# Hybrid encoder step on one Trainium2 core: low parts on VectorE, splits and sums issued ahead, the pooling mixer in two banks, filler matmuls in three norms

## What is computed

```python
h = rms_norm(x, norm_mix_g) * (1 + sc1) + sh1          # shift, scale, gate: silu(c) @ ada_w + ada_b
z = h @ w_in                                           # all mixers' inputs and the branch gates
oa = dsa_attention(...)   # indexer scores, top-k keys, softmax over them, 6 heads
ob = fox_attention(...)   # decay by cumulative sums of log-forget values, 6 heads
oc = pool_mixer(...)      # trailing means over 2, 4, 8, 16 frames minus the token, 64x64 map per group, scale
merged = sum_i sigmoid(gate_i) * (branch_i @ w_br_i)
x = x + g1 * (merged @ w_out)
h = rms_norm(x, norm_ffn_g) * (1 + sc2) + sh2
x = x + g2 * (swiglu(h) if layer == 0 else moe_ffn(h))  # moe: top 2 of 8 experts
```

## Time and profile before

| | |
|---|---|
| Runs | 2292.15, 2295.45, 2296.94 us |
| Profiled execution, its own time | 2291.52 us |
| Its span, first to last instruction | 2289.7 us |
| TensorE busy | 2173.7 us, 95% |
| Chain of work that ended last | TensorE 91%, VectorE 4%, DMA 2%, ScalarE 2%, issue 1% |
| VectorE / ScalarE / GpSimd busy | 34% / 25% / 13% |
| Mean granted TensorE clock | 0.964 of full speed |
| HBM traffic over the span | 147 GB/s |

### The profile page before, as it was taken

How to read it: one execution, slowest core, us unless ns; L and a number is a source line. 1 busy time by engine, 2 the same in 40 slices (tenths; PEclk the granted TensorE clock), 3 DMA queues, 4 the chain that set the end, 5 groups by cost and what they waited for, 6 DMA issues and landing times.

```text
span 2289.7 us, 38283 instructions
## 1 busy us (share of the span) xinstructions
PE 2173.7 (95%) x16051; PEld 2021.6 (88%) x16051; DVE 767.3 (34%) x1675; ACT 563.5 (25%) x1108; POOL 306.2 (13%) x194
## 2 busy tenths in 40 slices
PE   5999998999999999997999998999899999999995
PEld 3787998777989999997898997778699999999995
DVE  4032922545443333332308614545400000000024
ACT  4223321331232122223233312322411111111002
POOL 2223442000200000002224430003200000000001
PEclk8999998989999999998999998979999999999998
DMA  9674221501342243223624220012768877887783
GB/s 311 211 241 137 74 92 37 189 1 60 104 108 81 76 112 87 58 87 128 218 93 131 75 73 15 1 39 77 263 196 258 270 235 221 255 275 239 223 268 114
DMA packets 309445, 328.25 MB, mean 143 GB/s; under 512 B 7550, under 2 KB 276492, under 8 KB 308764
## 3 DMA queue, kind: packets, MB, share of 16 engines
q1 hardware_dynamic: 302144, 303.41, 42.1%
q0 software_dynamic: 5632, 18.41, 2.4%
q10 hardware_dynamic: 1548, 4.71, 0.5%
HBM read 310.29 MB, written 26.16 MB: 147 GB/s over the span
## 4 chain that ended last, share of the span: by engine, by line
PE 91%; DVE 4%; DMA 2%; ACT 2%; issue 1%; POOL 0%; DVEq 0%; SPq 0%; POOLq 0%; ACTq 0%
PE ps L1008 17%; PE ps L1363 17%; PE ps L1316 17%; PE ps L954 10%; PE ps L1344 8%; PE ps L881 5%; PE ps L1167 3%; PE ps L1153 3%; PE ps L1131 2%; PE ps L901 2%; PE ps L1073 1%; DMA slots<-in_ada_w 1%; PE ps L1391 1%; PE ps L1293 1%; PE ps L1328 1%
## 5 line engine op out<-in xcount | busy, mean ns | idle before, releaser
L1008 PE MATMUL ps<-hH,slotsR 128*128 128x272 f32 x1536 | 294.3, 291 | 3.9 <-ACT oT L1561 3.9
L1363 PE MATMUL ps<-hR,wR 128*128 128x272 f32 x2016 | 253.0, 288 | 1.8 <-DVE wR L2054 1.8
L1363 PEld LDWEIGHTS ps<-hR,wR 128*128 128x128 f32 x2016 | 252.7, 188 | 2.0 <-issue 2.0
L1008 PEld LDWEIGHTS ps<-hH,slotsR 128*128 128x128 f32 x1536 | 244.6, 191 | 4.5 <-issue 4.5
L730 POOL TENSOR_TENSOR slotsR<-slots,slotsR 128x1024 fp32r<-128x1024 f32 x64 | 154.9, 2440 | 610.8 <-ACT slotsR L1495 610.8
L1008 PE MATMUL ps<-hL,slotsR 128*128 128x272 f32 x768 | 223.3, 291 | 0.0
L954 PE MATMUL ps<-wz,hH 128*128 128x250 f32 (+1 forms) x680 | 194.8, 286 | 11.6 <-DVE hL L1779 7.3
L954 PE MATMUL ps<-slotsR,hH 128*128 128x250 f32 (+1 forms) x720 | 202.1, 281 | 0.0
L954 PE MATMUL ps<-wz,hL 128*128 128x250 f32 (+1 forms) x680 | 189.4, 279 | 0.0
L1316 PE MATMUL ps<-hg,slots 128*128 128x160 f32 x1280 | 177.3, 300 | 1.5 <-ACT hg L1657 0.6
L1316 PEld LDWEIGHTS ps<-hg,slots 128*128 128x128 f32 x1280 | 174.5, 190 | 3.5 <-issue 3.5
(11 more groups left out here) (364 smaller groups left out, 3399.6 us busy)
## 6 DMA issues: line engine op xcount, KB each, us to landing
slots<-in_w_in SPq DMA_DIRECT2D x24, 1024.0 KB, 5.2
slots<-in_ada_w SPq DMA_DIRECT2D x18, 1024.0 KB, 8.2
slots<-in_w_in SPq DMA_DIRECT2D x18, 1000.0 KB, 5.3
slots<-in_moe_w_gate SPq DMA_DIRECT2D x16, 1024.0 KB, 6.1
slots<-in_moe_w_up SPq DMA_DIRECT2D x16, 1024.0 KB, 8.0
w_more<-in_moe_w_gate SPq DMA_DIRECT2D x16, 1024.0 KB, 5.5
w_more<-in_moe_w_up SPq DMA_DIRECT2D x16, 1024.0 KB, 8.0
ada_x<-in_ada_w SPq DMA_DIRECT2D x15, 1024.0 KB, 7.1
```

What stands on the lines that cost most here:

```text
L1008: last = mm(ps[:, 2 * out_pair + a, 0:HALF], w[:, c], r[:, n], start=(k == i == 0), stop=(k == KD - 1 and i == 2))
L1363: last = mm(ps[:, 2 * out_pair + h, 0:HALF], wR[:, buf, a, k * P:(k + 1) * P], rhs(k, b)[:, c], start=(first and k == 0 and i == 0), stop= ...
```

## The change

1. **Start of layer 0.** The low parts of z block (0,0) move from GpSimd to VectorE (`proj_low`), at k = 1 and k = 4 of a loop that now interleaves `sample_affine` and `hidden_low`; ScalarE makes only the first half's high part ahead of norm 0 and the second after k = 2. The loads of `past` on GpSimd's queue move behind the low parts of block (0,1).
2. **z block (0,1), both layers.** ScalarE makes its high parts right after norm 2L.
3. **Layer 1's ada weights** take the three places in another order (3, 4, 5), so that the first fills wait for `x_upd` alone.
4. **Fillers.** `keep_busy` issues bf16 128x128 matmuls of an identity into bank 5, whose result is not read: 16 between the two halves of `norm_sums`, 14 ahead of `norm_scales`, 36 behind it, in norms 1, 2 and 3 (198 in all).
5. **Gates.** The wait for all 16 relu'd scores ahead of the first gate becomes 14 ahead of gate 0 and 16 ahead of gate 1.
6. **Pooling mixer.** Two buffers and two banks (5 and 6); VectorE copies tile t+1 before it scales tile t.
7. **Output product.** Its low parts move from GpSimd to VectorE (eight per layer), and `add_square(d-1)` stands ahead of `residual(d)` (in the FFN's second half too).
8. **End.** The second additions of token tiles 0 and 1 stand ahead of the last `y_copy`.

```diff
@@ buffers
-        pooled = qk[0:HD, 0:512]
+        pooled = [qk[0:HD, 0:512], oTf[0:HD, 1024:1536]]
@@ ada places
-        ... + [(5, 3, 4)[i % 3] for i in range(4 * ADA_LATER + 2 * ADA_FIRST)]
+        ... + [(5, 3, 4)[i % 3] for i in range(2 * (ADA_LATER + ADA_FIRST))] \
+            + [(3, 4, 5)[i % 3] for i in range(2 * ADA_LATER)]
@@ GpSimd
-                        low(("z", L), it, j)
+                        if L or it or j:
+                            low(("z", L), it, j)
+                        if L == it == 0 and j == 1:
+                            load_past()
...
-                with pool.Fori(0, 2) as it:
-                    for j in range(2):
-                        low(("out", L), it, j)
@@ TensorE, norm_sums and norm_scales
                     if i:
+                        if n:
+                            keep_busy(16)
                         pe.wait_ge(sq_ready, KD * (n + 1))
...
+            def keep_busy(count):
+                for _ in range(count):
+                    mm(ps[:, 5, 0:P], identb[:, :], identb[:, :], start=True, stop=True)
...
+                if n:
+                    keep_busy(14)
                 b0 = 2 * scale_pair(n)
...
                 last.then_inc(scale_ready, 1)
+                if n:
+                    keep_busy(36)
@@ TensorE, gates
-                pe.wait_ge(is_relu, 16 * (L + 1))
...
+                            if g < 2:
+                                pe.wait_ge(is_relu, 16 * L + 14 + 2 * g)
@@ TensorE, pooling mixer
+                pe.wait_ge(cum_evac, L + 1)
...
-                    if t:
-                        pe.wait_ge(po_evac, TILES * L + t)
+                    if t >= 2:
+                        pe.wait_ge(po_evac, TILES * L + t - 1)
...
-                            last = mm(ps[:, 5, pr * P:pr * P + r], poolw[:, g, :], pooled[:, g * P:g * P + r],
+                            last = mm(ps[:, 5 + t % 2, pr * P:pr * P + r], poolw[:, g, :], pooled[t % 2][:, g * P:g * P + r],
@@ ScalarE
-                    proj_high(("z", 0), 0, 0)
+                    proj_high(("z", 0), 0, 0, (0,))
...
-                norm(2 * L)
+                norm(2 * L, None if L else lambda: proj_high(("z", 0), 0, 0, (1,)))
+                proj_high(("z", L), 0, 1)
@@ VectorE
+            def proj_low(name, it, j, half):
+                high, low_part, w = proj_parts(name, j, it)
+                c = slice(half * 4 * w, (half + 1) * 4 * w)
+                dve.wait_ge(pw_high, proj_halves(name, it, j) + half)
+                V.tensor_tensor(low_part[:, c], slots[:, ring.slot(name, j), c], high[:, c].bitcast(FP), ALU.subtract)\
+                    .then_inc(pw_split, 1)
...
+                    for k in range(KD + 2):
+                        if k < KD:
+                            sample_affine(0, k)
+                        if k in (1, 4):
+                            proj_low(("z", 0), 0, 0, k // 4)
+                        if k >= 2:
+                            hidden_low(0, k - 2)
...
+                    if d >= KD - 2:
+                        proj_low(("out", L), 0, 0, d - (KD - 2))
                 merged_low(KD - 1)
+                for half in range(2):
+                    proj_low(("out", L), 0, 1, half)
...
+                    if d:
+                        add_square(2 * L + 1, d - 1)
                     dve.wait_ge(r_ready, KD * L + d + 1)
                     residual(d % 4, d, M_G1)
-                    if d:
-                        add_square(2 * L + 1, d - 1)
+                    if d in (1, 3):
+                        for half in range(2):
+                            proj_low(("out", L), 1, d // 2, half)
...
                     for d in range(KD):
+                        if d == KD - 1:
+                            add_second(0, 0)
+                            add_second(0, 1)
                         y_copy(before, d)
```

More of the change, by code:

```diff
@@ L518, in proj_parts @@
             return slotsR[:, 3 - j % 2, :], slotsR[:, j % 2, :], 2 * P
-        ada_places = [0, 1, 2, 3, 4, 5, 3, 4] + [(5, 3, 4)[i % 3] for i in range(4 * ADA_LATER + 2 * ADA_FIRST)]
+        ada_places = [0, 1, 2, 3, 4, 5, 3, 4] + [(5, 3, 4)[i % 3] for i in range(2 * (ADA_LATER + ADA_FIRST))] \
+            + [(3, 4, 5)[i % 3] for i in range(2 * ADA_LATER)]
         def ada_chunk(n):
@@ L718, in _, with load_past @@
                     pool.wait_ge(ot_evac, L * NTM)
[L719 to L721 removed]
+                def load_past():
+                    pool.dma_start(past[:, 0:192], t_in["cache_a_kvi"][L, 0].rearrange("t c d -> t (c d)")).then_inc(past_loaded, 16)
+                    pool.dma_start(past[:, 192:960], t_in["cache_b_kv"][L, 0].rearrange("t c h d -> t (c h d)")).then_inc(past_loaded, 16)
+                    pool.dma_start(past[:, 960:966], t_in["cache_b_logf"][L, 0]).then_inc(past_loaded, 16)
+                if L:
+                    load_past()
                 def low(name, it, j):
@@ L927, in _ @@
                     pe.wait_ge(vt_evac, 2)
+                    pe.wait_ge(memsets, 3)
                 def indexer_columns(i):
@@ L1460, in ffn_high, with norm @@
                 A(wR[:, w, 0, 0:n], slots[:, j % NSLOT, c0:c0 + n], ACT.Copy).then_inc(w_high, 1)
-            def norm(n):
+            def norm(n, weights_too=None):
                 act.wait_ge(mod_ready, n + 1)
@@ L1480, in norm @@
                         high(k - 1)
+                    if weights_too and k == 2:
+                        weights_too()
                 if n < 3:
@@ L1484, in _, with proj_high @@
             for L in range(DEPTH):
-                def proj_high(name, it, j):
+                def proj_high(name, it, j, parts=(0, 1)):
                     high, _, w = proj_parts(name, j, it)
@@ L1492, in proj_high @@
                         act.wait_ge(block_begun, released)
-                    for half in range(2):
+                    for half in parts:
                         c = slice(half * 4 * w, (half + 1) * 4 * w)
@@ L1837, in _ @@
                     ada_finish(0, 0, 16, ADA_FIRST)
-                    for k in range(KD):
-                        sample_affine(0, k)
-                    for k in range(KD):
-                        hidden_low(0, k)
+                    for k in range(KD + 2):
[5 more added lines that the diff above has]
+                            hidden_low(0, k - 2)
                 tmpf = oT[:, :, :].rearrange("p k n -> p (k n)")
@@ L1953, in _ @@
                 last.then_inc(cum_evac, 1)
-                for t in range(TILES):
-                    r = ROWS[t]
-                    dve.wait_ge(pm_ready, TILES * L + t + 1)
-                    if t:
-                        dve.wait_ge(po_ready, TILES * L + t)
-                    v4 = lambda ap: ap.rearrange("p (g n) -> p g n", g=4)[:, :, 0:r]
-                    V.tensor_copy(v4(pooled), v4(ps[0:HD, t, :])).then_inc(pm_evac, 1)
-                    dve.wait_ge(po_ready, TILES * L + t + 1)
-                    for pr in range(2):
-                        last = V.tensor_scalar(oT[:, 6 + pr, tok(t)], ps[:, 5, pr * P:pr * P + r],
-                                               vecT[:, L, V_PSC + pr:V_PSC + pr + 1], None, ALU.mult)
-                    last.then_inc(po_evac, 1)
+                for t in range(TILES + 1):
+                    if t < TILES:
+                        r = ROWS[t]
+                        dve.wait_ge(pm_ready, TILES * L + t + 1)
+                        if t >= 2:
+                            dve.wait_ge(po_ready, TILES * L + t - 1)
+                        v4 = lambda ap: ap.rearrange("p (g n) -> p g n", g=4)[:, :, 0:r]
+                        V.tensor_copy(v4(pooled[t % 2]), v4(ps[0:HD, t, :])).then_inc(pm_evac, 1)
+                    if t:
+                        b, r = t - 1, ROWS[t - 1]
+                        dve.wait_ge(po_ready, TILES * L + b + 1)
+                        for pr in range(2):
+                            last = V.tensor_scalar(oT[:, 6 + pr, tok(b)], ps[:, 5 + b % 2, pr * P:pr * P + r],
+                                                   vecT[:, L, V_PSC + pr:V_PSC + pr + 1], None, ALU.mult)
+                        last.then_inc(po_evac, 1)
                 for i, (kind, t) in enumerate(at_groups):
@@ L2240, in _ @@
                         if d >= 0:
+                            if it and d:
+                                add_square(2, d - 1)
                             dve.wait_ge(unit_done[1], it * nb + (n0 * nb + FB + d + 1))
@@ L2243, in _ @@
                             residual((d + 2) % 4, d, M_G2)
-                            if it and d:
-                                add_square(2, d - 1)
                     if it + 1 < HALVES:
                         ffn_low(it + 1, 0, 0)
+                    else:
+                        add_square(2, KD - 2)
                     dve.wait_ge(unit_done[1], it * nb + (n0 * nb + FB + KD))
```

22 lines of the change are left out of this document (10 added, 12 removed).

## The result

The changed kernel takes 2270.15 us (median of four runs, 2263.33 to 2273.15) against 2296.19 us for the kernel before beside it; the ratio is 0.9873 with a 95% interval of 0.9856 to 0.989, that is 25 to 33 us less. Two later sets of runs of the same kernel gave 0.9884 (0.9867 to 0.99) and 0.9886 (0.9864 to 0.9908). The forecast was 2262 in a range of 2249 to 2275, from a sum of -31.6; the sign and the range held, the time lies 8 us above the forecast, and by the medians (26.0, 28.0 and 25.5 us less in the three sets) the sum was 4 to 6 us too large.

The account below looks back on a forecast made before the run. TensorE, busy 95% of the span, was taken as the bound, so only its waits and half-clock stretches pay; terms summed to -31.6 from 2291.5 us, 2259.9, plus 2 gives 2262, range 2249 to 2275.

Parts of the forecast that it names:

- the third rival: Norms 1 to 3: fillers only cost, clock comes back no earlier; +4.4 instead of -3.8 us, 2270; chance 0.13.
- the second rival: Pooling mixer stays at half clock, products 2.07, transposes gain nothing; -5.6 instead of -16.2 us, 2273; chance 0.15.
- Pooling mixer, -16.2: Two buffers let VectorE and TensorE work side by side at full clock; -8.1 us in each layer, -16.2.
- Start, -2.7: Start of layer 0: first z product at 46.6 instead of 49.7; -2.7 us, between -1.5 and -3.1.
- z block (0,1) and ada fill: Earlier high parts end waits for GpSimd's low parts, -3.7 us; layer 1's ada fill issued earlier, -2.2.
- Gates, -1.9: Two waits for ScalarE's last relu, 3.9 us, are halved: -1.9 us, between 0 and -3.9.
- Output product, -2.0: TensorE starts 2.3 us earlier per layer, less late low part and residual 2; net -2.0, between -4.6 and +1.
- Norms, -3.8: Norms 1 to 3: fillers restore the clock before the products, -6.7, cost 0.9 and 2.0; net -3.8 us.
- The base case: Norms 1 to 3: clock still falls in the sums; 36 fillers restore it by the first product; forecast chance 0.43.
- the first rival: Norms 1 to 3: fillers hold the clock throughout, scales too at full speed; -9.7 us, 2256; chance 0.24.
- End, +0.9: Last `y_copy` stands behind two additions that wait for gathers; +0.9 us, between 0 and +1.4.
- The rival on the other side: VectorE's queue blocks the output product if a transfer lands later; 20 us later gives 2302; chance 0.02.

Follow-up runs that it names:

- the three traces: Changed kernel, no edit: the trace shown with the result and those of two repeats; ratios 0.9873, 0.9884 and 0.9886 to the kernel before.
- the repeat: Changed kernel a third time, no edit, against the kernel before: ratio 0.9886 (0.9864 to 0.9908).
- seven traces: Changed kernel's three, plus mixer in one bank (0.9943), mixer fillers (0.9889), other output-product order (0.9871), second additions behind last copy (0.9881).
- three traces of eight: Changed kernel's three traces and five runs keeping the moved additions; the three: no fillers (0.9882), first wait filled (0.9852), mixer filled (0.9889).

## Why the prediction was right, and where its steps were off

The sign and the range held, but the sum did not. By the stages the three traces show -20.7, -20.3 and -16.6 against -31.6, and the errors hardly cancel: only the norms with layer 1's z block gave clearly more than forecast, and only in two traces; the other misses are smaller gains or larger losses. The medians show more than the traces (25.5 to 28.0); it fits that the trace of before, which the sum was made against, is of one of its fastest executions. The time is inside the range by the range's width: 2270 is also what the third rival gives, and the second rival gives 2273. So the number by itself shows none of the three right; the stages have to.

- **Pooling mixer, -16.2: mis-sized.** It measured -10.9 to -12.0 by the stages. The step that failed is "TensorE's pauses shrink from 1.29 to 0.12 us, so I take full clock". The clock fell there in every trace of the changed kernel with TensorE nearly always busy ahead of it, and only with fillers between its products did it hold. The rival for this case had its price too high as well (-5.6): the clock falls only at the third product, so two tiles run at full speed, and the stage takes 7.2 to 8.1, not 10.8. The mechanism was the rival's, the size lay between the two, and the transposes gave back nothing, as the rival said.
- **Start, -2.7: right in kind.** It measured -2.8 in the repeat whose norm 0 ran at full clock, and -0.9 to -1.0 in the two whose norm 0 took two microseconds more for its 20 one-column sums, which no edit touches. Of the twelve traces with this start nine have -2.4 to -3.0. L1769's successor takes 289 to 301 ns in the three traces, which fits that the 2.40 of the earlier trace rows was GpSimd's subtraction.
- **z block (0,1) and ada fill: right for layer 1,** 5.0 against 5.2 without fillers. Layer 0's 0.7 does not show (-0.1, -0.1, +0.5). Its waits did shrink: the 1.2 us for GpSimd are gone, and the ada transfers took back 0.7 of it (2.0 us of waits instead of 1.3; the forecast had 0.6). But the first products now start earlier in the half clock and have 4.5 to 5.9 us of it instead of the 3.1 of the earlier trace rows, which costs 0.7 to 1.4 more.
- **Gates, -1.9: right,** 0.9 a layer.
- **Output product, -2.0: mis-sized, and the sign with it.** TensorE started 3.05 us earlier where the stage ahead ran at full clock (44.10 instead of 47.15), and the product then took 3.2 more: +0.2 a layer. The rest of the +1.8 to +4.5 is half clock that the stage ahead has in some traces and layers (45.6 to 46.9). The two stalls were named in the prediction, but at 0.5 and 0.8 instead of 1.0 and 1.7. The first was sized without the chain behind it: TensorE wants the second low half at 567.2, while five steps of VectorE, of which the half is the last, follow the branches' last product and end at 568.15; the second lacked the 0.75 us that TensorE took to go on once the residual was there (1.0 late where 0.7 was worked out). The new order of the low halves and of residual 1 removes 2.1 to 2.6 us a layer, so the place was right and the term mis-sized.
- **Norms, -3.8: not shown by the time.** By the stages the fillers bring from 5.0 us to a loss of 0.4, 2.4 in the mean of seven traces against one without them. Another 0.7 a norm in norms 1 to 3 comes from the sums' earlier start, which was no term of the sum and is there without fillers too. The base case described norms 2 and 3; norm 1 went the way of the first rival in two traces of three, and in three of the seven. The Trainium skill, "TensorE: Matmul & The Clock Gate", Part 1, "What's actually happening", would have had activity release the clock. In norm 3 the trace agrees only where the first wait is filled too, and there in one trace of three (17.76 with no half clock; 19.38 with 3.4 us of it, 20.12 with 6.8).
- **End, +0.9: right in three traces of eight, too small in five** (+2.2 to +3.1, the three of the table among them). The bound of +1.4 counted one pair of additions where two were moved; and the waits for the gathers (2.45 and 0.50), which depend on how far ahead of the copy the gathers are issued, were not in it. The Trainium skill, "SBUF — State Buffer", section "SBUF: two separate sides", has a GpSimd transfer wait for VectorE's use of the shared port. The trace shows 1.23 for the fourth gather, issued beside an addition, against 0.95 to 0.97 for the three ahead of it; but the copy waits only for the first two, which were issued before any addition ran, so that rule adds nothing to its lateness.
- **The rival on the other side** did not come: VectorE's queue held TensorE for 2.7 us a layer, not for eighteen.

The prediction's own signs agree with this account: the sign of the second rival came (products of 1.85 to 1.91, where it names 2.07), while the 5 us a layer without which the forecast was to fall were just met in that stage (5.6 to 6.4).

What stays open: why the clock falls in norm 1 in one execution and not in another, and what sets how far ahead of the last copy the gathers are issued. No run controls either.

## What to carry to other kernels

A pause that is removed does not by itself bring the clock back: read the granted clock of the stretch after the change, and price a stage at both levels. When work moves to the engine whose queue also frees the banks, list what stands behind each new wait in order, and put the part that TensorE needs first in front of it; and where a wait goes, work out which result the waiting engine asks for next, and when it comes. Where single executions differ by some microseconds, cut the trace into stages and compare those over several traces, since the total hides gains and losses of 3 us alike.

## What the runs showed of the hardware that was not expected

One-column fp32 matmuls follow the clock too: norm 0's 20 sums, in the first trace of the changed kernel and then in its third:

```profile
26.47 4.42 PE L867 MATMUL ps<-ones,z 128*128 128x1 f32 x20 [2.44 <-DVE z L1818]
```

```profile
26.68 2.39 PE L867 MATMUL ps<-ones,z 128*128 128x1 f32 x20 [2.24 <-DVE z L1818]
```

0.22 us each against 0.12, in a part of the program that no edit touches. The same kernel on the same data falls to half clock at different places: norm 1 not at all in two traces and for 3.4 us in the third, norm 3 for 6.8, 10.2 and 10.2 us, and attention for 24 to 31 us in every trace of both kernels. That is larger than most edits here are worth. And half clock came in the pooling mixer with TensorE busy 4.75 of 5.0 us ahead of it and no pause longer than 0.40:

```profile
376.00:381.00 5.00, 4.75 (x48) 4.35 (x46) 3.68 (x8) 0.00 (x0) 1.45 (x1) 1.00 0.00 0
```
